# Merge gates of a decoder layer in seven block products instead of eight, product by product, with the sums of weight pieces on VectorE

## The chip, the cores and the metric

One NeuronCore of one Trainium2 chip. The metric is device time in microseconds of one execution; lower is better. TensorE is called PE here, VectorE DVE, ScalarE ACT, GpSimd POOL, and SP is the engine that issues most DMAs.

## The reference

One decoder layer on 1024 tokens of width 1024. What the change touches is the merge of two branches:

```python
qa, ka, va, qb, kb, vb, gb, gate_a, gate_b = jnp.split(h @ w_in[l], split_idx, axis=-1)
ya = oa.reshape(B, S, DA_WIDTH) @ w_branch_a[l]
yb = (jax.nn.silu(gb) * ob) @ w_branch_b[l]
merged = jax.nn.sigmoid(gate_a) * ya + jax.nn.sigmoid(gate_b) * yb
x = x + merged @ w_out[l]
```

Ahead of it stand differential attention (4 heads) and retention (4 heads), behind it the output projection and a mixture of 32 experts.

## The kernel before

Every fp32 product is made of three: each operand is a high part (fp32r, an ACT copy) and a low part (value minus high part, a DVE subtraction), and `split3` (L109 to L115) issues high by high, low by high and high by low, each a matmul over 512 columns. The normed input stands turned in SBUF as `hTH[th]` and `hTL[th]` (high and low; th is the half of the tokens, 512 of them, and the 8 pieces k of 128 channels stand in each).

Four stages follow each other on PE. **Heads** (`head_steps`): four heads, each with 8 steps of attention (A) and 8 of retention (B) in a pipeline over token tiles. In the last steps of the last head (16 to 18), where no projection is left, `first_gates` (L640) fills 48 matmuls of the next stage in between: the gates of unit 0. **Gates and branches**: 16 units s, each a slab m = s % 8 of 128 output channels and a half th = s // 8 of the tokens. A unit is `gates(s)` (L815: 2 gates x 8 pieces x 3 matmuls) and `branches(s)` (L824: 2 branches x 4 pieces x 3). Its weights, 1.5 MB in four transfers (`load_C`, L502), go to one of two buffers `wC_in`; ACT copies them to `wCH` in three pieces of 128x1024 (`high_C`, L1046), DVE makes `wCL` (`low_C`, L1512). ACT then takes the tanh of both gates out of PSUM (L1211), DVE multiplies each by its branch (L1752) and adds the two (L1755) into `merged`. **Output projection**: 16 products of 24 matmuls each, with the router's small ones in between. **Experts**: 192 weight pieces of 1 MB, split by ACT and DVE.

Within an engine the order of the instructions is the order of the program text; engines wait for each other by semaphores only. Each engine has its own loop over the units. DVE's is: the three `low_C` of unit s + 1, then the three operations on unit s. POOL does nothing in the gate stage but one small product on the router's weights.

Of the kernel before, what the change touches and what calls it, by code (L numbers as in the profile page):

```python
# [8 lines left out]
ALU = mybir.AluOpType  # L9
# [46 lines left out]

MAGIC = 1.5 * 2.0 ** 23
# [51 lines left out]
def split3(pe, out, left, right, start, stop):  # L109


    (lh, ll), (rh, rl) = left, right
    pe.matmul(out, lh, rh, start=start, stop=False)  # L113
    pe.matmul(out, lh, rl, start=False, stop=False)  # L114
    return pe.matmul(out, ll, rh, start=False, stop=stop)  # L115


def decoder_layer(nc, T):
    with ExitStack() as ctx:
# [87 lines left out]
        oTH = sb("oTH", [P, 8, 512], F32R, at=oTH_at)  # L207
# [99 lines left out]
        def pick(t, c):  # L307
# [30 lines left out]
        slot_at = [R_HT, R_HT + 16 * KIB, R_WORK, R_B, R_B + 16 * KIB, R_OT, R_OT + 16 * KIB, merged_at[1],  # L338
                   R_HT + 32 * KIB, R_HT + 48 * KIB]
# [43 lines left out]
        def x_bank(i, half):  # L383
# [3 lines left out]
        names = """pos_in first_turned x_next wA_first late_in g1_in consts_in gains_in small_in x_again x_in0 x_in1 x_in2 x_in3 x_sq_done x_ms_done x_rstd_done  # L387
# [20 lines left out]
        PREP_C = {3: 0, 5: 1, 6: 2}  # L408
        PREP_T = {12: 0, 15: 1, 16: 2, 17: 3}
# [47 lines left out]
        def _(sp):  # L457
# [1582 lines left out]
```

## Time and profile before

| | |
|---|---|
| median of 3 runs | 1454.28 us (1452.56 to 1455.19) |
| span of the profiled execution | 1451.4 us |
| PE busy | 1423.0 us (98%), 7361 matmuls |
| DVE busy | 998.9 us (69%) |
| ACT busy | 827.7 us (57%) |
| POOL busy | 412.0 us (28%) |

The profile gives the span, from the first to the last instruction of the profiled execution; a time of that execution on the scale of the runs is not given apart from it. The median lies 2.9 us above the span. A matmul's recorded duration overlaps the next one's, so how fast PE goes is read from start to start.

### The profile page before, as it was taken

Reading aid. Unit: us, or ns where it says so; the run is one execution under the profiler, and the core shown is the slowest. Engines: PE = TensorE matmul, PEld = TensorE weight load, DVE = VectorE, ACT = ScalarE, POOL = GpSimd, SP = SyncE. Lnnn points to the kernel's source line nnn. Section 1 sums busy time; section 2 is a strip of 40 time slices with the busy share of each in tenths; the row PEclk is TensorE's granted clock in tenths of the full one; section 3 lists DMA queues with packets and bytes.
Section 4 is the critical chain, followed back from the end, with each engine's and each line's share of the span. In section 5 each row is a group of like instructions: output and inputs, shape, how many; then the busy total and the mean of one; then the engine's idle time right before and its main releaser. Section 6 shows DMA issues by size and latency. Waiting matters only on the chain.

```text
span 1451.4 us, 19659 instructions
## 1 busy us (share of the span) xinstructions
PE 1423.0 (98%) x7361; PEld 1203.3 (83%) x7362; DVE 998.9 (69%) x1440; ACT 827.7 (57%) x1349; POOL 412.0 (28%) x463
## 2 busy tenths in 40 slices
PE   6999999999999999999999999999999999999997
PEld 5888988988988888888888878888888888888885
DVE  7855754764664533435332558999999999999996
ACT  5643453453453322324233238888888888888883
POOL 3325324424424300000000112233333333333331
PEclk9999999999999999999999999999999999999999
DMA  5211110210210333463340549999999999999991
GB/s 178 56 45 35 28 44 2 62 44 1 63 45 1 88 87 88 114 167 88 87 183 6 216 168 421 405 384 386 386 388 382 398 383 402 399 393 404 398 405 52
DMA packets 132946, 285.94 MB, mean 197 GB/s; under 512 B 17897, under 2 KB 96881, under 8 KB 108274
## 3 DMA queue, kind: packets, MB, share of 16 engines
q1 hardware_dynamic: 119296, 263.58, 49.7%
q0 software_dynamic: 13248, 21.00, 3.9%
q8 instruction: 60, 0.98, 0.3%
q14 instruction: 36, 0.29, 0.1%
q10 hardware_dynamic: 306, 0.07, 0.0%
HBM read 286.70 MB, written 25.17 MB: 215 GB/s over the span
## 4 chain that ended last, share of the span: by engine, by line
PE 95%; DVE 2%; issue 1%; POOL 1%; DMA 0%; ACT 0%; POOLq 0%; SPq 0%; DVEq 0%
PE proj L113 18%; PE proj L115 18%; PE proj L114 18%; PE scores L113 7%; PE scores L115 7%; PE scores L114 7%; PE scores L719 2%; PE outs L796 2%; PE scores L588 2%; PE turned L113 1%; PE turned L115 1%; PE turned L114 1%; PE turned L588 1%; PE outs L890 1%; PE turned L759 1%
## 5 line engine op out<-in xcount | busy, mean ns | idle before, releaser
L1839 DVE TENSOR_TENSOR w_low<-w_slot,w_high 128x2048 fp32r<-128x2048 f32 x192 | 430.8, 2286 | 0.1
L1243 ACT ACTIVATE w_high<-w_slot 128x2048 fp32r<-128x2048 f32 x190 | 349.5, 1906 | 2.6 <-DMA w_slot<-in_w_up 2.6
L113 PE MATMUL proj<-w_high,xeH 128*128 128x512 f32 x512 | 202.1, 395 | 0.3 <-DVE xeL L1945 0.3
L115 PE MATMUL proj<-w_high,xeL 128*128 128x512 f32 x512 | 200.0, 391 | 0.0
L114 PE MATMUL proj<-w_low,xeH 128*128 128x512 f32 x512 | 199.6, 390 | 0.0
L1451 POOL DMA_INDIRECT out<-y,ids_rows x31 | 86.6, 2792 | 338.2 <-DVE y L1961 338.2
L1048 ACT ACTIVATE wCH<-wC_in 128x1024 fp32r<-128x1024 f32 x48 | 47.7, 1052 | 152.0 <-DMA wC_in<-in_w_branch_b 152.0
L1515 DVE TENSOR_TENSOR wCL<-wC_in,wCH 128x1024 fp32r<-128x1024 f32 x48 | 57.2, 1243 | 90.0 <-ACT wCH L1048 90.0
L115 PEld LDWEIGHTS proj<-w_high,xeL 128*128 128x128 f32 x512 | 96.1, 188 | 20.1
L113 PEld LDWEIGHTS proj<-w_high,xeH 128*128 128x128 f32 x512 | 96.6, 189 | 19.4 <-issue 0.4
L114 PEld LDWEIGHTS proj<-w_low,xeH 128*128 128x128 f32 x512 | 96.3, 188 | 19.1
L113 PE MATMUL proj<-wBH,hTH 128*128 128x512 f32 x256 | 111.9, 437 | 0.0
L115 PE MATMUL proj<-wBH,hTL 128*128 128x512 f32 x256 | 101.0, 395 | 0.0
L113 PE MATMUL proj<-wAH,hTH 128*128 128x384 f32 x256 | 98.6, 385 | 2.0 <-DVE wAL L1510 2.0
L114 PE MATMUL proj<-wBL,hTH 128*128 128x512 f32 x256 | 100.4, 392 | 0.0
L113 PE MATMUL scores<-w_high,hidH 128*128 128x512 f32 x248 | 99.7, 402 | 0.0
L115 PE MATMUL scores<-w_high,hidL 128*128 128x512 f32 x248 | 97.0, 391 | 0.0
L114 PE MATMUL scores<-w_low,hidH 128*128 128x512 f32 x248 | 96.7, 390 | 0.0
L115 PE MATMUL proj<-wAH,hTL 128*128 128x384 f32 x256 | 87.0, 340 | 0.0
L114 PE MATMUL proj<-wAL,hTH 128*128 128x384 f32 x256 | 86.7, 339 | 0.0
L1251 ACT ACTIVATE xs<-scores,small 128x128 f32<-128x128 f32 x256 | 70.0, 384 | 10.4 <-PE scores L588 6.1
L1439 POOL DMA_INDIRECT xe<-x_rows,ids_rows x32 | 59.5, 1860 | 24.2 <-DVE ids_rows L1862 9.6
(317 smaller groups left out, 3181.2 us busy)
## 6 DMA issues: line engine op xcount, KB each, us to landing
w_slot<-in_w_gate SPq DMA_DIRECT2D x64, 1024.0 KB, 8.1
w_slot<-in_w_up SPq DMA_DIRECT2D x64, 1024.0 KB, 8.0
w_slot<-in_w_down SPq DMA_DIRECT2D x64, 1024.0 KB, 7.8
wC_in<-in_w_in SPq DMA_DIRECT2D x32, 512.0 KB, 5.2
wB_in<-in_w_in SPq DMA_DIRECT2D x16, 512.0 KB, 6.4
wA_in<-in_w_in SPq DMA_DIRECT2D x9, 512.0 KB, 6.0
wC_in<-in_w_branch_a SPq DMA_DIRECT2D x16, 256.0 KB, 5.6
wC_in<-in_w_branch_b SPq DMA_DIRECT2D x16, 256.0 KB, 5.5
```

Source lines behind the costliest of these rows:

```text
L113: pe.matmul(out, lh, rh, start=start, stop=False)
L114: pe.matmul(out, lh, rl, start=False, stop=False)
L115: return pe.matmul(out, ll, rh, start=False, stop=stop)
L588: last = pe.transpose(dst[:, k * 128:(k + 1) * 128], src_rows[:, DS(k, 128, step=step)], ident)
L719: pe.matmul(SC[:, c, t0 * 128:t1 * 128], q_part[r, 0, :], k_part[r, 1 + t0:1 + t1, :].rearrange("p a b -> p (a b)"), start=q_part is qkTH ...
L1048: act.activation(wCH[sub][:, piece * 8:piece * 8 + 8, :], wC_in[sub][:, piece * 8:piece * 8 + 8, :], ACT.Copy).then_inc(S["wC_high"], 1)
L1243: act.activation(w_high[slot][:], w_in6[slot][:], ACT.Copy).then_inc(S["w_split"], 1)
L1251: act.activation(xs[:, k, :], SC[:, 0, k * 128:(k + 1) * 128], ACT.Copy, scale=g2x[:, k:k + 1]).then_inc(S["xs_done"], 1)
L1439: pool.indirect_dma_start(out=xe[j % 4][:], out_offset=None, in_=x2_dram, in_offset=ids_of(ids_rows, j), bounds_check=1023, oob_is_err=Fal ...
L1451: pool.indirect_dma_start(out=out_rows, out_offset=ids_of(ids_rows, j), in_=rows[:], in_offset=None, bounds_check=1023, oob_is_err=False). ...
L1515: dve.tensor_tensor(wCL[sub][:, r, :], wC_in[sub][:, r, :], wCH[sub][:, r, :].bitcast(F32), ALU.subtract).then_inc(S["wC_low"], 1)
L1839: dve.tensor_tensor(w_low[slot][:], w_in6[slot][:], w_high[slot][:].bitcast(F32), ALU.subtract).then_inc(S["w_lows"], 1)
```

## The change

The 2 x 8 x 2 gate products are regarded as one product of 2x2 blocks: the weights' blocks are (gate a, gate b) by (channels 0 to 511, 512 to 1023), the input's are (channels 0 to 511, 512 to 1023) by (tokens 0 to 511, 512 to 1023). Strassen's scheme computes the four result blocks from seven block products M1 to M7 in place of eight. Each is cut into 8 slabs m, so there are 56 products o of 4 pieces x 3 matmuls, listed in `GATE_PRODUCTS`: M5, M2, M1 with their 8 slabs each, then M3 and M6 in groups of four (M3 i, M3 i+1, M6 i, M6 i+1), then M4 and M7 the same way. Products 0 to 3 take the place of unit 0 in the last head. `branches` follow, all 16, each slab and half as before.

The weight operand of a product is the sum or difference of two blocks (M3 and M4: one block), made by DVE (`operand_sum(o)`, for the first six `early_sum(o)` inside the last head), with its high copy by ACT (`high_operand`) and its low part by DVE (`low_operand`). There are four buffers for operands and three for raw rows of 512 KB. The input operand is a block for M5 and M2, and a sum of blocks for the others: s1 for M1 is summed inside the last head (`sum_s1`), s3, s4, s6 and s7 in two halves each in the gate stage (`half_sum(u)` and `half_split(u)` on DVE, u = 0 to 7). Of such a sum POOL makes the sum of the low parts (`half_lows(u)`), DVE that of the high parts and then the sum of both. The results leave PSUM by ACT copies (M5, M2) or DVE additions (`add_product`: two for M1, one for the others); M6 and M7 are accumulated onto what their bank holds, which M3 or M4 left there. Buffers move: four weight buffers of 1 MB for the branches, `x2` and two of the experts' slots in other places.

```diff
+SINGLES, PAIRS = ("M5", "M2", "M1"), (("M3", "M6"), ("M4", "M7"))
+GATE_PRODUCTS = [(kind, m) for kind in SINGLES for m in range(8)]
+for _one, _two in PAIRS:
+    for _i in range(0, 8, 2):
+        GATE_PRODUCTS += [(_one, _i), (_one, _i + 1), (_two, _i), (_two, _i + 1)]
...
+ROW_OF = {"M5": 0, "M2": 8, "M1": 16, "M3": 24, "M6": 24, "M4": 32, "M7": 32}
+PLAIN = ("M3", "M4")
+BANK_OF = (1, 3, 4, 5, 0, 2, 6, 7)
+EARLY_SUMS, FILLED = 6, 4
...
+SUM_AT = {9: 0, 10: 1, 12: 2, 13: 3, 16: 4, 17: 5}
+S1_SUM_AT = {11: 0, 14: 1, 15: 2, 16: 3}
...
+            def load_gate(r):
...
+                pieces = (((GATE_A, 0), (GATE_A, 4)), ((GATE_B, 0), (GATE_B, 4)), ((GATE_A, 0), (GATE_B, 4)),
+                          ((GATE_A, 0), (GATE_B, 0)), ((GATE_B, 4), (GATE_A, 4)))[kind]
+                for j, (col, k) in enumerate(pieces):
+                    sp.dma_start(gate_raw[r % 3][:, j, :, :], w_in_v[:, k:k + 4, col + m * 128:col + m * 128 + 128]
+                                 ).then_inc(S[f"w_land{r % 3}"], DMA)
+
...
+            def gate_part(o, k):
+
+                (kind, m), slot = GATE_PRODUCTS[o], o % 4
+                high, low_ = right[kind]
+                added = kind in ("M6", "M7")
+                last = split3(pe, bank(BANK_OF[m]), (gate_high[slot][:, k, :], gate_low[slot][:, k, :]),
+                              (high[:, k, :], low_[:, k, :]), k == 0 and not added, k == 3, added)
+                if k == 3:
+                    last.then_inc(S["c_done"], 1)
+
+            first_pieces = [(o, k) for o in range(FILLED) for k in range(4)]
 
...
+            for o in range(FILLED, N_GATE):
+                kind, m = GATE_PRODUCTS[o]
...
+                if kind in ("M2", "M1"):
+                    pe.wait_ge(S["gate_out"], PLACE["M5" if kind == "M2" else "M2", m] + 1)
+                elif kind in ("M3", "M6", "M4", "M7"):
+                    before_it = {"M3": "M1", "M6": "M3", "M4": "M6", "M7": "M4"}[kind]
+                    pe.wait_ge(S["merged_step"], gate_adds(PLACE[before_it, m]))
...
+                    pe.wait_ge(S["h_low"], 4)
+                if m == 0 and kind in ("M3", "M4", "M6", "M7"):
+                    pe.wait_ge(S["h_low"], 4 + {"M3": 2, "M4": 4, "M6": 6, "M7": 8}[kind])
+                pe.wait_ge(S["wC_low"], o + 1)
+                for k in range(4):
+                    gate_part(o, k)
+                if o == 5:
+                    pe.wait_ge(S["t_free"], N_HEADS * T_ROUND - 1 + FREE)
...
+            def branches(s):
+                th, slot = s // 8, s % N_WC
+                tok = slice(th * 512, th * 512 + 512)
+                pe.wait_ge(S["wC_low"], N_GATE + s + 1)
+                if s < 4:
+                    pe.wait_ge(S["merged_step"], gate_adds(PLACE["M7", 2 * s + 1]))
+                else:
+                    pe.wait_ge(S["merged_step"], GATE_ADDS + 2 * (s - 4) + 2)
...
+            high_operand(6)
+            high_operand(7)
+            act.wait_ge(S["gTB"], 8 * N_HEADS + FREE)
+            act.activation(oT[:, N_HEADS + 3, 7 * 128:8 * 128], TB[:, 0:128], ACT.Copy, scale=0.25).then_inc(S["t_free"], 1)
+            for o in range(4):
+                copy_product(o)
+            for o in range(8, N_GATE):
+                if o - 4 < PLACE["M1", 0]:
+                    copy_product(o - 4)
+                high_operand(o)
+                if o in (9, 10, 12, 13, 16, 17, 30, 31):
+                    high_half((9, 10, 12, 13, 16, 17, 30, 31).index(o))
+                if o in (40, 42, 44, 46):
+                    high_turned((o - 40) // 2, 0)
+                if o >= 44 and o % 2 == 0:
+                    gate_tanh(0, (o - 44) // 2)
+            high_C(0)
+            high_C(1)
...
+            def half_lows(u):
+
+                s, ks = ("s3", "s4", "s6", "s7")[u // 2], slice(u % 2 * 2, u % 2 * 2 + 2)
...
+                    pool.wait_ge(S["h_low"], 4 + u % 2 + 1)
+                    pool.wait_ge(S["h_low"], 4)
+                    one, two, op = h_low["s1"], h_low["s3"], ALU.add
+                if s == "s7":
+                    pool.wait_ge(S["c_done"], PLACE["M2", 7] + 1)
...
+                pool.tensor_tensor(h_lows[s][:, ks, :], one[:, ks, :].bitcast(F32), two[:, ks, :].bitcast(F32), op
+                                   ).then_inc(S["h_lows"], 1)
+
+            for u in range(8):
+                half_lows(u)
...
+            def early_sum(o):
+
+                dve.wait_ge(S[f"w_land{o % 3}"], 2 * DMA * (o // 3 + 1))
+                if o >= 4:
+                    dve.wait_ge(S["c_done"], o - 3)
+                dve.tensor_tensor(gate_sum[o % 4][:], gate_raw[o % 3][:, 0, :, :], gate_raw[o % 3][:, 1, :, :], ALU.add
+                                  ).then_inc(S["h_step"], 1)
+
+            def low_operand(o):
+
+                (kind, m), slot = GATE_PRODUCTS[o], o % 4
+                whole = gate_raw[(ROW_OF[kind] + m) % 3][:, 0, :, :] if kind in PLAIN else gate_sum[slot][:]
+                dve.wait_ge(S["wC_high"], o + 1)
...
+            def sum_s1(k):
+
+                s = h_raw["s1"][:, k, :]
+                dve.tensor_tensor(s, b11[0][:, k, :].bitcast(F32), b22[0][:, k, :].bitcast(F32), ALU.add).then_inc(S["h_step"], 1)
+                for n, part in enumerate((b11[1], b22[1])):
+                    dve.wait_ge(S["h_step"], STEPS_TO[f"s1_{k}"] - 2 + n)
+                    dve.tensor_tensor(s, s, part[:, k, :].bitcast(F32), ALU.add).then_inc(S["h_step"], 1)
...
+            def half_sum(u):
+
+                s, ks = ("s3", "s4", "s6", "s7")[u // 2], slice(u % 2 * 2, u % 2 * 2 + 2)
...
+                raw = h_raw[s][:, ks, :]
+                dve.tensor_tensor(raw, one[:, ks, :].bitcast(F32), two[:, ks, :].bitcast(F32), op).then_inc(S["h_step"], 1)
+                dve.wait_ge(S["h_step"], S1_STEPS + 2 * u + 1)
+                dve.wait_ge(S["h_lows"], u + 1)
+                dve.tensor_tensor(raw, raw, h_lows[s][:, ks, :], ALU.add).then_inc(S["h_step"], 1)
+
+            def half_split(u):
+
+                s, ks = ("s3", "s4", "s6", "s7")[u // 2], slice(u % 2 * 2, u % 2 * 2 + 2)
...
+            def add_product(o):
+
+                kind, m = GATE_PRODUCTS[o]
+                a0, a1, b0, b1 = merged[0][:, m, :], merged[1][:, m, :], gateB[0][:, m, :], gateB[1][:, m, :]
+                dve.wait_ge(S["c_done"], o + 1)
+                if kind == "M1":
+                    dve.wait_ge(S["gate_out"], PLACE["M2", m] + 1)
+                    dve.tensor_tensor(a1, bank(BANK_OF[m]), a0, ALU.subtract).then_inc(S["merged_step"], 1)
+                    dve.tensor_tensor(b0, bank(BANK_OF[m]), b1, ALU.subtract).then_inc(S["merged_step"], 1)
+                    return
+                into = {"M3": a0, "M6": b0, "M4": b1, "M7": a1}[kind]
+                dve.wait_ge(S["merged_step"], 2 * m + 2)
+                dve.tensor_tensor(into, bank(BANK_OF[m]), into, ALU.add).then_inc(S["merged_step"], 1)
+
+            def operand_sum(o):
+
+                (kind, m), slot = GATE_PRODUCTS[o], o % 4
+                r = ROW_OF[kind] + m
+                dve.wait_ge(S[f"w_land{r % 3}"], 2 * DMA * (r // 3 + 1))
+                dve.wait_ge(S["c_done"], o - 3)
+                one, two = gate_raw[r % 3][:, 0, :, :], gate_raw[r % 3][:, 1, :, :]
+                if kind in ("M6", "M7"):
+                    dve.tensor_tensor(gate_sum[slot][:], two, one, ALU.subtract).then_inc(S["gate_sums"], 1)
+                else:
+                    dve.tensor_tensor(gate_sum[slot][:], one, two, ALU.add).then_inc(S["gate_sums"], 1)
...
+            operand_sum(6)
+            for o in range(6, N_GATE):
+                if o + 1 < N_GATE and GATE_PRODUCTS[o + 1][0] not in PLAIN:
+                    operand_sum(o + 1)
+                low_operand(o)
+                if o - 4 >= PLACE["M1", 0]:
+                    add_product(o - 4)
+                if o in (8, 9, 11, 12, 14, 15, 28, 29):
+                    half_sum((8, 9, 11, 12, 14, 15, 28, 29).index(o))
+                if o in (10, 11, 13, 14, 17, 18, 31, 32):
+                    half_split((10, 11, 13, 14, 17, 18, 31, 32).index(o))
+                if o in (41, 43, 45, 47):
+                    low_turned((o - 41) // 2, 0)
+            low_C(0)
+            low_C(1)
+            for o in range(N_GATE - 4, N_GATE):
+                add_product(o)
```

How the change moves DVE's program. Before, one unit in the second half (three low parts of the next unit, two multiplications, one addition, three low parts):

```order
L1515 TENSOR_TENSOR wCL0_108<-wC_in0_106,wCH0_110 128x1024 [waits wC_high] x3
L1752 SCALAR_TENSOR_TENSOR sig_116<-sig_116,scores 128x512 [waits ys_done,sig_tanh]
L1752 SCALAR_TENSOR_TENSOR sig_116<-sig_116,scores 128x512
L1755 TENSOR_TENSOR merged1_113<-sig_116 128x512 [waits merged_step]
L1515 TENSOR_TENSOR wCL1_109<-wC_in1_107,wCH1_111 128x1024 [waits wC_high] x3
```

Now, on DVE, from the sum of product 9 to the low part of product 10 (`s3_raw` and `s3L` are halves of the input sum s3; `gate_sum`, `gate_high`, `gate_low` are operands of weights):

```order
L1984 TENSOR_TENSOR gate_sum1_117<-gate_raw0_113 128x512 [waits c_done,w_land0]
L1699 TENSOR_TENSOR gate_low0_120<-gate_sum0_116,gate_high0_124 128x512 [waits wC_high]
L1948 TENSOR_TENSOR s3_raw_128<-hTH0_51 128x1024 [waits projB]
L1951 TENSOR_TENSOR s3_raw_128<-s3_raw_128,s3_lows_132 128x1024 [waits h_lows,h_step]
L1984 TENSOR_TENSOR gate_sum2_118<-gate_raw1_114 128x512 [waits c_done,w_land1]
L1699 TENSOR_TENSOR gate_low1_121<-gate_sum1_117,gate_high1_125 128x512 [waits wC_high]
L1948 TENSOR_TENSOR s3_raw_128<-hTH0_51 128x1024 [waits projB]
L1951 TENSOR_TENSOR s3_raw_128<-s3_raw_128,s3_lows_132 128x1024 [waits h_lows,h_step]
L1984 TENSOR_TENSOR gate_sum3_119<-gate_raw2_115 128x512 [waits c_done,w_land2]
L1699 TENSOR_TENSOR gate_low2_122<-gate_sum2_118,gate_high2_126 128x512 [waits wC_high]
L1957 TENSOR_TENSOR s3L_140<-s3_raw_128,s3H_136 128x1024 [waits h_high]
```

Between the two pieces for one product stand the halves of the input sums, whole 128x1024 operations. POOL, after its last step of the last head (before, the next row after `gatedR` was the router's `wr`):

```order
L1543 TENSOR_TENSOR gatedR_102<-onR_101,sg_96 128x128 [waits sg_done,gTB,gate_step]
L1585 TENSOR_TENSOR s3_lows_132<-hTL0_53 128x1024 [waits projB] x2
L1585 TENSOR_TENSOR s4_lows_135<-hTL1_54 128x1024 x2
L1585 TENSOR_TENSOR s6_lows_133<-s1L_146,s3L_140 128x1024 [waits h_low,h_step,c_done] x2
L1585 TENSOR_TENSOR s7_lows_134<-s4L_143,s1L_146 128x1024 [waits h_low,h_step,c_done] x2
L1592 TENSOR_TENSOR wr_172<-wr_172,g2_cols_174 128x288 [waits router_in]
```

Eight 128x1024 operations stand there, each of which a DVE addition waits for through `h_lows`. DVE again, from the low part of product 32 to the addition of product 30 (groups of M3 and M6; `proj0` and `proj1` are the banks of slabs 2 and 3):

```order
L1699 TENSOR_TENSOR gate_low0_120<-gate_raw1_114,gate_high0_124 128x512 [waits wC_high]
L1972 TENSOR_TENSOR merged0_105<-proj0,merged0_105 128x512 [waits merged_step,c_done]
L1957 TENSOR_TENSOR s7L_142<-s7_raw_130,s7H_138 128x1024 [waits h_high]
L1982 TENSOR_TENSOR gate_sum2_118<-gate_raw1_114 128x512 [waits c_done,w_land1]
L1699 TENSOR_TENSOR gate_low1_121<-gate_raw2_115,gate_high1_125 128x512 [waits wC_high]
L1972 TENSOR_TENSOR merged0_105<-proj1,merged0_105 128x512 [waits merged_step,c_done]
L1982 TENSOR_TENSOR gate_sum3_119<-gate_raw2_115 128x512 [waits c_done,w_land2]
L1699 TENSOR_TENSOR gate_low2_122<-gate_sum2_118,gate_high2_126 128x512 [waits wC_high]
L1972 TENSOR_TENSOR gateB0_109<-proj0,gateB0_109 128x512 [waits merged_step,c_done]
```

The sum of product 34 (`gate_sum2` in the fourth row, which waits for the end of product 30 by `c_done`) and the low part of product 33 now stand ahead of the addition of product 29 on `proj1`, for which PE waits through `merged_step` before it begins product 31 on the same bank.

## Rows read from the trace of the kernel before

**Rows 1.** The page: span, busy time of each engine, the chain's shares.
```profile
span 1451.4 us, 19659 instructions
...
PE 1423.0 (98%) x7361; PEld 1203.3 (83%) x7362; DVE 998.9 (69%) x1440; ACT 827.7 (57%) x1349; POOL 412.0 (28%) x463
...
PE 95%; DVE 2%; issue 1%; POOL 1%; DMA 0%; ACT 0%; POOLq 0%; SPq 0%; DVEq 0%
```

**Rows 2.** The waits of PE: released line, releaser; total us, times, longest.
```profile
PE scores L627 <- DVE x_all L1666: 5.4, 3, 3.8
```

**Rows 3.** Windows: busy us (instructions) of PE, PEld, DVE, ACT, POOL; clock; DMA share; GB/s.
```profile
492.30:742.70 250.40, 250.40 (x1106) 207.40 (x1106) 96.52 (x101) 71.56 (x86) 4.12 (x4) 1.00 0.37 98
...
900.00:950.00 50.00, 50.00 (x236) 41.85 (x235) 47.76 (x29) 43.15 (x42) 16.06 (x7) 1.00 1.01 405
```

**Rows 4.** The tile wCH: count, duration min/median/max in ns, first and last start.
```profile
L113 PE MATMUL proj<-hTH,wCH x128: 388/389/482, 479.4 to 720.3; 128*128 128x512 f32 x128
...
L113 PE MATMUL scores<-hTH,wCH x128: 388/389/390, 497.9 to 742.0; 128*128 128x512 f32 x128
```

**Rows 5.** Timeline of PE in the gate stage: start, us, instruction.
```profile
492.30 0.40 PE L113 MATMUL turned<-oTH,wCH 128*128 128x512 f32 x1
...
497.70 0.39 PE L115 MATMUL outs<-oTH,wCL 128*128 128x512 f32 x1
...
519.01 0.39 PE L113 MATMUL proj<-hTH,wCH 128*128 128x512 f32 x1
...
523.09 0.39 PE L113 MATMUL proj<-hTH,wCH 128*128 128x512 f32 x1
...
742.73 0.39 PE L113 MATMUL proj<-wDH,mergedH 128*128 128x512 f32 x1
```

**Rows 6.** Timeline of DVE, end of the last head and the gate stage.
```profile
469.12 1.22 DVE L1515 TENSOR_TENSOR wCL<-wC_in,wCH 128x1024 fp32r<-128x1024 f32 x1
...
475.72 1.51 DVE L1515 TENSOR_TENSOR wCL<-wC_in,wCH 128x1024 fp32r<-128x1024 f32 x1
...
491.33 1.22 DVE L1521 TENSOR_TENSOR oTL<-oT,oTH 128x1024 fp32r<-128x1024 f32 x1
...
498.23 0.69 DVE L1752 SCALAR_TENSOR_TENSOR sig<-sig,turned 128x512 f32<-128x512 f32 x1 [0.39 <-PE outs L115]
...
498.84 0.68 DVE L1752 SCALAR_TENSOR_TENSOR sig<-sig,outs 128x512 f32<-128x512 f32 x1
...
499.55 0.69 DVE L1755 TENSOR_TENSOR merged<-sig 128x512 f32<-128x512 f32 x1
...
506.74 3.50 DVE L1515 TENSOR_TENSOR wCL<-wC_in,wCH 128x1024 fp32r<-128x1024 f32 x3 [6.50 <-ACT wCH L1048]
```

**Rows 7.** Timeline of POOL, the same stretch, and its one large product at 623.6.
```profile
475.69 0.46 POOL L1389 TENSOR_TENSOR onR<-onR,gn_rows 128x128 f32<-128x128 f32 x1 [0.53 <-DVE onR L1624]
...
476.23 1.33 POOL L1391 TENSOR_TENSOR onR<-onR,gn_rows 128x128 f32<-128x128 f32 x1
...
623.62 1.77 POOL L1418 TENSOR_TENSOR wr<-wr,g_cols 128x288 f32<-128x288 f32 x1 [128.81 <-DMA small<-in_norm_g]
```

**Rows 8.** Timeline of DVE around 621.
```profile
621.37 3.50 DVE L1515 TENSOR_TENSOR wCL<-wC_in,wCH 128x1024 fp32r<-128x1024 f32 x3 [2.38 <-ACT wCH L1048]
```

**Rows 9.** Groups of POOL by form: count, busy us, mean ns.
```profile
L1395 POOL TENSOR_TENSOR gatedR<-onR,sg 128x128 f32<-128x128 f32 x32 | 15.6, 488 | 2.5
...
L1424 POOL TENSOR_TENSOR ms<-ms,ssq 128x1 f32<-128x1 f32 x8 | 1.5, 190 | 51.0 <-ACT x_sq L1218 51.0
```

**Rows 10.** Groups of ACT by form.
```profile
L1048 ACT ACTIVATE wCH<-wC_in 128x1024 fp32r<-128x1024 f32 x48 | 47.7, 1052 | 152.0 <-DMA wC_in<-in_w_branch_b 152.0
...
L1211 ACT ACTIVATE sig<-proj 128x512 f32<-128x512 f32 x16 | 8.7, 594 | 2.2 <-PE proj L115 2.2
```

**Rows 11.** Windows after the last output product, where the granted clock falls.
```profile
862.00:863.00 1.00, 1.00 (x6) 1.00 (x6) 0.86 (x7) 0.62 (x3) 0.00 (x0) 0.50 0.00 0
```

**Rows 12.** The page: DMA issues, KB each, median us to landing.
```profile
wC_in<-in_w_in SPq DMA_DIRECT2D x32, 512.0 KB, 5.2
```

More of the change, by code:

```diff
@@ L247, in decoder_layer @@
-        wD_at = [R_HT, R_B]
+        raw_at = [R_A, R_A + 4 * KIB, R_WORK + 16 * KIB]
+        gate_raw = [sb(f"gate_raw{i}", [P, 2, 4, 128], F32, at=raw_at[i]) for i in range(3)]
+        gate_sum = [sb(f"gate_sum{i}", [P, 4, 128], F32, at=R_A + (8 + 4 * i) * KIB) for i in range(4)]
+        gate_low = [sb(f"gate_low{i}", [P, 4, 128], F32R, at=R_A + (8 + 4 * i) * KIB) for i in range(4)]
+        gate_high = [sb(f"gate_high{i}", [P, 4, 128], F32R, at=R_A + (10 + 4 * i) * KIB) for i in range(4)]
@@ new lines, in _, with high_merged @@
+            high_C(0)
+            high_C(1)
+            gate_tanh(0, 6)
+            gate_tanh(0, 7)
+            def high_merged(i):
+                act.activation(mergedH[i // 4][:, :, i % 4 * 128:(i % 4 + 1) * 128], merged[i // 4][:, :, i % 4 * 128:(i % 4 + 1) * 128],
+                               ACT.Copy).then_inc(S["mH"], 1)
+            for s in range(N_UNITS):
+                if s + 2 < N_UNITS:
+                    high_C(s + 2)
+                if s == 0:
+                    act.wait_ge(S["c_done"], N_GATE)
+                if s < 4:
+                    high_turned(s, 1)
+                if s < 8:
+                    gate_tanh(1, s)
+                if s in (8, 9):
+                    high(wDH[0][s - 8][:], wD_in[0][:, (s - 8) * 4:(s - 8) * 4 + 4, :], S["w_land7"], DMA, S["wD_high"])
+                if s in (10, 11, 12, 13):
+                    act.wait_ge(S["sig_mul"], 8)
+                    high_merged(s - 10)
@@ L1213, in square_half @@
+            act.wait_ge(S["sig_mul"], N_UNITS)
+            for i in range(4, N_TILES):
+                high_merged(i)
             def square_half(cnt):
@@ L1747, in _ @@
-                if s == 0:
-                    dve.wait_ge(S["gated"], 8 * N_HEADS + FREE)
-                dve.wait_ge(S["sig_tanh"], 2 * s + 2)
-                dve.wait_ge(S["ys_done"], s + 1)
-                for g in range(2):
-                    dve.scalar_tensor_tensor(sig[:, g, :], sig[:, g, :], 1.0, bank(b0 + 2 + g), ALU.add, ALU.mult
+                m, th = s % 8, s // 8
+                if s + 2 < N_UNITS:
+                    low_C(s + 2)
+                if s < 4:
+                    low_turned(s, 1)
@@ new lines, in _ @@
+                if s in (9, 10):
+                    low(wDL[0][:, (s - 9) * 4:(s - 9) * 4 + 4, :], wD_in[0][:, (s - 9) * 4:(s - 9) * 4 + 4, :], wDH[0][s - 9][:],
+                        S["wD_high"], s - 8, S["wD_low"])
+                if s in (11, 12, 13, 14):
+                    low_merged(s - 11)
+                dve.wait_ge(S["gate_out"], 16 + 2 * s + 2)
+                dve.wait_ge(S["c_done"], N_GATE + s + 1)
+                for g, gate in enumerate((merged[th], gateB[th])):
+                    dve.scalar_tensor_tensor(gate[:, m, :], gate[:, m, :], 1.0, bank(BANK_OF[(2 * s + g) % 8]), ALU.add, ALU.mult
```

361 lines of the change are left out of this document (205 added, 156 removed).

## The prediction

> **What bounds the kernel now.** I read the page first: PE is busy for 98% of the span and is 95% of the chain that ended last [rows 1]. Busy time alone proves little, since matmuls overlap in the records, so the waits of PE come next: the longest, 5.4 us in all, is for the first tiles at the start [rows 2], and in the gate stage there is none. The windows say the same: from 492.3, where the first matmul after `first_gates` starts, to 742.73, where the output projection starts [rows 5], PE is busy throughout at a granted clock of 1.00 (2.4 GHz), while DVE works 96.5 us of 250.4, ACT 71.6 and POOL 4.1 [rows 3]. So PE's instructions are the bound there, and the others have room on average. The timeline gives the price of a matmul: 18 of them lie between the starts at 519.01 and 523.09 [rows 5], so 0.2267 us each; a block product of 12 takes 2.72 us. The experts' stage has PE full too [rows 3], and nothing in its program changes, so what is won or lost before it should reach the end.
>
> **Term 1, the matmuls removed.** Gates: 256 issues each of three kinds, 768 [rows 4]. After: 56 x 12 = 672. 96 x 0.2267 = **-21.8 us**. The 48 that are filled into the last head stay 48, so PE is at product 4 at 492.3 as now [rows 5]. If nothing else waited, product 17 would start at 492.3 + 13 x 2.72 = 527.7.
>
> **Prices on DVE and POOL.** A 128x512 of DVE takes 0.69, but the next can start 0.61 later (498.23 to 498.84) [rows 6]. A 128x1024 takes 1.22, with 1.14 from start to start: three in 3.50 [rows 6]. An operation that waits for its predecessor's result starts at its end (498.84 + 0.68, next at 499.55). POOL has no 128x1024 in the trace. Its sum of one column takes 0.19 and its product of 128 columns 0.49 at mean, 0.46 undisturbed [rows 7, 9], so 2.1 ns a column and 0.19 + 1024 x 0.0021 = 2.4 us. The product of 288 columns took 1.77 from 623.62, of which DVE's third piece of that moment ran until about 624.8 [rows 7, 8], which leaves 0.6 us for 288 columns; in proportion 0.6 x 1024 / 288 = 2.1. The lower bound is 1.3 (a line through 0.46 at 128 and 0.6 at 288), the upper 8 x 0.46 = 3.7. I take 2.1, from the largest operation.
>
> **What POOL's work costs DVE.** At 475.69 POOL starts a 0.46 us operation, at 475.72 DVE a 128x1024, which takes 1.51 instead of 1.22; POOL's next, begun at 476.23 beside it, takes 1.33 instead of 0.46 and ends just behind it [rows 6, 7]. Each is held up while the other runs, nearly for its whole length. So I charge DVE all of a POOL operation that meets a full DVE queue: 2.1 us each. The other reading, a fixed cost of 1.51 - 1.22 = 0.29 per POOL operation, is the lower bound. The Trainium skill (SBUF — State Buffer, Who interferes with whom) says that a DVE instruction with two SBUF inputs contends with a GpSimd one that reads SBUF, as an exclusive lock held for the whole instruction. By that rule eight operations cost DVE 8 x 2.1 = 16.8 us, by the fixed cost 2.3; it speaks against giving POOL these sums. The two rows agree with it.
>
> **Term 2, DVE in front of products 6 to 17.** The last piece that DVE does in the last head starts at 491.33 [rows 6]; two small ones take its place, so its loop over the products starts near 492.7, with products up to 5 prepared. Until the low part of product 17, which PE needs, it has: 13 sums and 12 low parts at 0.61, 15.3; six halves of input sums, each an addition and a second that waits for it, 1.22 + 0.04 + 1.14 = 2.40, 14.4; four low halves at 1.14, 4.6; eight POOL operations at 2.1, 16.8; and some 1.2 us at the start, since raw row 7 is fetched only after a sum in step 16 and lands 5.2 us later [rows 12] (an estimate). Sum 52.3, so 545.0 against PE's 527.7: PE is late by **+17.3 us**. All eight POOL operations fall there: the first four follow the last head at once, two follow the low halves of s3, and the last two wait only for product 15. The operands' four buffers cannot hide it: they hold DVE back when it is early, not the reverse. ACT's share here (a copy from PSUM, a high part, at times a 1.05 us half: at most 2.3 us per 2.72) fits [rows 10]. DMA fits too: 512 KB per 2.72 us, three rows ahead, landing in 5.2.
>
> **Term 3, PE behind an addition in the groups of M3/M6 and M4/M7.** In the second product of M6 (or M7) in each group PE accumulates on a bank that DVE's addition of M3 (or M4) must have read. In DVE's program that addition stands behind the sum for a product of the next group, which waits until PE has finished the very product before. So PE stops each time for: the end and the signal of its last matmul, 0.53 (497.70 to 498.23 [rows 5, 6]), the sum 0.61, the low part 0.61, the addition 0.69, some 0.05 for the signal, less the 0.23 after which PE would have gone on: 2.2 to 2.3 us. Eight groups, of which the last has no sum of a next group behind it: 7 x 2.2 = 15.4. Where ACT's or DVE's larger pieces stand ahead of an addition (before products 26, 30, 42, 46 and 54) I add 2.3 in all: **+17.7 us**. DVE has caught up by then: from product 18 to 23 it needs 4 x 0.61 = 2.4 per product against 2.72. Bounds: 1.4 per stop (only low part and addition behind PE's signal) and 2.7.
>
> **Edits at nothing.** The pieces inside the last head: a step there lasts longer than its DVE work, and the new ones (at most five 128x512, 3.4 us, in step 16) take the place of one 1.22 us piece; if a following step is pushed, up to +1.5 us. The branches alone: a unit of 24 matmuls is 5.44 us, DVE's share at most 1.14 + 2 x 1.14 + 1.9 = 5.3. Output projection: its first split weights and `merged` parts are made in units 8 to 14, before PE gets there. The x2 and experts' buffers have other places, but wait for the same events.
>
> **Sum.** -21.8 + 17.3 + 17.7 = +13.2. The profiled span would become 1451.4 + 13.2 = 1464.6, and the median 1454.3 + 13.2 = **1467.5 us**.
>
> **The rivals.**
> 1. POOL's operations cost DVE little (0.29 each, or 2.1 that fall into idle time). Then DVE has 52.3 - 16.8 + 2.3 = 37.8 us to do until 530.5; PE is late by 3, or by up to 6 where the halves come bunched: -21.8 + 4.5 + 17.7 = +0.4 to +2 and at most +3.5; about 1456. For it: POOL has waits of its own between its operations. Against: the two rows of 475.7.
> 2. It gets faster. The place is the addition in the groups: if it is out in time, because sums run ahead of the signals I charge, term 3 falls to a few tenths. With term 2 full that is -21.8 + 17.3 + 2 = -2.5 (1451.8); with rival 1 too, -21.8 + 4.5 + 2 = -15.3 (1439). It decides when the addition can be done 0.2 us after the product before. The order of the program speaks against it.
> 3. The clock. After the last output product PE did only small work with gaps, and the granted clock fell to 0.50 (1.2 GHz) at 862 [rows 11]. In the stretch before product 17 PE would work about 2.72 of each 4 us, with gaps of up to 4 us. A product at the lower level takes 5.44; against DVE's pace that loses up to 1.8 each, and three such products 5 us, outside the stretch 2.7 each: +13.2 + 5 to + 10, so 1473 to 1478. The Trainium skill (TensorE: Matmul & The Clock Gate, Part 1: The HAM clock gate) says that the clock goes to 1.2 GHz once PE has been idle and comes back with sustained work; by that rule the longest gaps could cost these 5 us, and without it nothing. I leave the clock out of the sum, since matmuls fill most of the stretch.
>
> **How the numbers follow.** Two tenths of a per cent, 2.9 us, is about what a measurement of this kernel tells from no change. Forecast (terms 2 and 3 both there): 0.65. Rival 1: 0.15, of which half stays within 0.2%. Rival 2: 0.04 on its slight side, 0.05 on its large side. Rival 3: 0.11. Slower by over 0.2%: 0.65 + 0.11 + 0.08 = 0.84. Within: 0.07 + 0.02 = 0.09. Faster: 0.02 + 0.05 = 0.07. The range: POOL at 1.3 takes 6.4 off (1461), stops of 1.4 another 5.6 (1455.5), which is also rival 1's middle; POOL at 3.7 adds 12.8 (1480), with a little clock 1483. So 1455 to 1483.
>
> **What would show it.** In the profile after: POOL rows of 128x1024 near 2.1 us or longer, DVE pieces of 128x512 that last 2 to 3 us between 495 and 545, and PE waits for `gate_low` before products 7 to 17, 15 to 20 us in all. Then seven PE waits of about 2.2 us for DVE's addition, every fourth product from 27 to 51, some 13 us apart. From the output projection on, all as before, 13 us later. It is wrong if PE shows no wait there, if the POOL rows don't lengthen DVE's, or if waits stand somewhere else, as at a DMA row or in the branches.

## The result, and the profile after

The changed kernel takes **1475.04 us** (median of 4 runs, 1473.78 to 1475.23) against 1454.58 (4 runs, 1452.56 to 1455.19): a ratio of 1.0142, 95% interval 1.0128 to 1.0157. It is slower by 20.5 us, where 13.2 were forecast.

The page of the changed kernel, span, busy times and the chain:

```profile
span 1473.3 us, 19883 instructions
...
PE 1414.3 (96%) x7265; PEld 1189.8 (81%) x7266; DVE 1108.3 (75%) x1592; ACT 849.2 (58%) x1401; POOL 431.7 (29%) x471
...
PE 89%; DVE 7%; issue 2%; ACT 1%; POOL 0%; DMA 0%; ACTq 0%; DVEq 0%; POOLq 0%
```

PE has 96 matmuls fewer than in [rows 1], and DVE has gone from 2% of the chain to 7%. The waits of PE (us in total, times, longest) say where:

```profile
PE scores L154 <- DVE gate_low L1699: 10.6, 5, 3.9
PE turned L154 <- ACT oT L1321: 5.9, 1, 5.9
PE scores L154 <- DVE merged L1972: 4.3, 3, 2.1
PE scores L154 <- DVE gateB L1972: 4.3, 3, 2.1
...
PE proj L154 <- DVE gateB L1972: 2.2, 2, 2.1
PE proj L154 <- DVE merged L1972: 2.2, 2, 2.1
PE outs L154 <- DVE merged L1972: 2.1, 1, 2.1
```

None of these stood in the gate stage before. The five groups for L1972, DVE's addition, hold seven stops of 2.06 us and four small ones. Windows over products 4 to 17, products 17 to 55 with their additions, and the branches (columns as in [rows 3]):

```profile
494.00:551.00 57.00, 41.58 (x159) 32.15 (x160) 54.69 (x47) 22.34 (x37) 23.41 (x11) 0.88 0.46 129
551.00:678.00 127.00, 111.22 (x470) 88.04 (x469) 81.58 (x121) 40.32 (x63) 1.43 (x1) 0.99 0.34 96
678.00:765.00 87.00, 87.00 (x385) 72.04 (x384) 59.68 (x70) 33.25 (x39) 0.00 (x0) 1.00 0.42 133
```

In the first, DVE is busy for 54.7 of 57 us: it is the bound there. In the second nobody is full, so what costs time is the order of the work. In the third PE is full again: the branches take 87.04 us, 384 matmuls at the forecast 0.2267.

The first window's POOL and DVE, side by side. Timeline of POOL:

```profile
496.34 10.66 POOL L1585 TENSOR_TENSOR s_lows<-hTL 128x1024 f32<-128x1024 f32 x4
520.62 2.62 POOL L1585 TENSOR_TENSOR s_lows<-s1L,s3L 128x1024 f32<-128x1024 f32 x1 [13.62 <-DVE s3L L1957]
527.55 2.57 POOL L1585 TENSOR_TENSOR s_lows<-s1L,s3L 128x1024 f32<-128x1024 f32 x1 [4.31 <-DVE s3L L1957]
544.58 5.37 POOL L1585 TENSOR_TENSOR s_lows<-s4L,s1L 128x1024 f32<-128x1024 f32 x2 [14.46 <-PE outs L156]
```

Timeline of DVE:

```profile
496.76 2.50 DVE L1699 TENSOR_TENSOR gate_low<-gate_sum,gate_high 128x512 fp32r<-128x512 f32 x1 [0.70 <-ACT gate_high L1157]
499.18 2.87 DVE L1711 TENSOR_TENSOR s1L<-s_raw,s1H 128x512 fp32r<-128x512 f32 x1
501.97 5.58 DVE L1984 TENSOR_TENSOR gate_sum<-gate_raw 128x512 f32<-128x512 f32 x2
507.47 0.68 DVE L1699 TENSOR_TENSOR gate_low<-gate_sum,gate_high 128x512 fp32r<-128x512 f32 x1
...
520.31 0.68 DVE L1984 TENSOR_TENSOR gate_sum<-gate_raw 128x512 f32<-128x512 f32 x1
520.91 2.88 DVE L1699 TENSOR_TENSOR gate_low<-gate_sum,gate_high 128x512 fp32r<-128x512 f32 x1
523.71 1.21 DVE L1948 TENSOR_TENSOR s_raw<-hTH 128x1024 f32<-128x1024 f32 x1
```

While POOL works, the same 128x512 of DVE takes 2.9 us instead of 0.68: each POOL operation (2.4 to 2.8 us) takes some 2.2 us from DVE. The loop's first sum starts at 501.97. Further on, DVE and PE at the first of the seven stops:

```profile
576.72 1.23 DVE L1951 TENSOR_TENSOR s_raw<-s_raw,s_lows 128x1024 f32<-128x1024 f32 x1
578.73 0.69 DVE L1982 TENSOR_TENSOR gate_sum<-gate_raw 128x512 f32<-128x512 f32 x1 [0.79 <-PE scores L156]
579.33 0.69 DVE L1699 TENSOR_TENSOR gate_low<-gate_raw,gate_high 128x512 fp32r<-128x512 f32 x1
579.94 0.69 DVE L1972 TENSOR_TENSOR merged<-scores,merged 128x512 f32<-128x512 f32 x1
```

```profile
578.23 0.39 PE L156 MATMUL scores<-s6H,gate_low 128*128 128x512 f32 x1
580.67 0.50 PE L154 MATMUL scores<-s6H,gate_high 128*128 128x512 f32 x1 [2.06 <-DVE merged L1972]
```

DVE itself is idle before the sum, which waits for PE's product 26; then sum, low part and addition follow, and only the last is what PE waits for.

### The profile page after: what moved, and what is told of

Read it like the earlier page. It is cut to its first block, busy times and chain, and to the rows that moved or that the text cites. A ratio compares the mean times of both kernels' runs of the same rounds, so it can differ in the third digit from the quotient of the medians.

```text
span 1473.3 us, 19883 instructions
## 1 busy us (share of the span) xinstructions
PE 1414.3 (96%) x7265; PEld 1189.8 (81%) x7266; DVE 1108.3 (75%) x1592; ACT 849.2 (58%) x1401; POOL 431.7 (29%) x471
## 4 chain that ended last, share of the span: by engine, by line
PE 89%; DVE 7%; issue 2%; ACT 1%; POOL 0%; DMA 0%; ACTq 0%; DVEq 0%; POOLq 0%
PE proj L154 17%; PE proj L156 17%; PE proj L155 17%; PE scores L154 6%; PE scores L156 6%; PE scores L155 6%; PE scores L813 2%; PE outs L890 2%; PE scores L670 2%; DVE gate_low L1699 2%; PE turned L154 1%; PE turned L156 1%; PE turned L155 1%; PE turned L670 1%; PE outs L988 1%
## 5 line engine op out<-in xcount | busy, mean ns | idle before, releaser
L1157 ACT ACTIVATE gate_high<-gate_sum 128x512 fp32r<-128x512 f32 x40 | 25.4, 635 | 87.6 <-DVE gate_sum L1982 53.2
```

## The experiments

Each ratio compares with runs of the kernel before on the same chip. These had medians of 1454.6 us beside the change, 1453.5 beside e1 to e4, 1454.0 beside e5 and e6 and 1452.5 beside e7 to e9, so a difference in us between kernels of two such groups is uncertain by 1 to 2 us. For the stretches, the starts of PE's products in each profiled execution: from product 4 to product 17 (PE alone: 13 x 2.72 = 35.4 us), and from product 17 to the branches' first matmul (39 x 2.72 = 106.1). In the ten profiled executions of changed kernels product 0 starts between 478.05 and 479.89 us, so a stretch is a better measure than a position.

```
kernel                    median us   ratio to before   products 4-17   17-branches
before                    1454.6      -                 -               -
the change                1475.0      1.0142            56.2            127.1
e1 additions first        1455.8      1.0014            56.2            107.6
e2 lows on VectorE        1469.2      1.0106            49.0            127.6
e3 lows as fills          1460.7      1.0044            41.9            128.2
e4 = e1 + e2              1450.2      0.9979            50.4            110.0
e5 = e4, spread           1450.5      0.9978            38.3            121.6
e6 = e5, one at a time    1435.9      0.9873            36.7            107.6
e7 = e6, lows on GpSimd   1443.9      0.9932            43.8            109.0
e8 = e6, additions back   1457.9      1.0029            36.7            129.3
e9 s1 of high parts only  1474.9      1.0144            53.9            130.7
```

**The additions put first.**

```diff
             for o in range(6, N_GATE):
+                if o - 4 >= PLACE["M3", 0]:
+                    add_product(o - 4)
                 if o + 1 < N_GATE and GATE_PRODUCTS[o + 1][0] not in PLAIN:
                     operand_sum(o + 1)
                 low_operand(o)
-                if o - 4 >= PLACE["M1", 0]:
+                if PLACE["M1", 0] <= o - 4 < PLACE["M3", 0]:
                     add_product(o - 4)
```

> The additions of products 24 to 51 are put ahead of the next weight sum on VectorE (nothing else moves). Theory (term 3: the stops at products 27, 31, ... 51 come from the addition standing behind a sum that itself waits for the bank): the seven stops of 2.06 us idle and the small ones go, 21.0 us between product 17 and the branches become 3 to 6; 1475.0 - 16 = 1459 us (1456 to 1462). Rival (VectorE is short of time there anyway, so the wait only changes its name): within 3 us of 1475.

1455.76 us (1454.04 to 1457.10, 11 runs), ratio 1.0014 (1.0005 to 1.0022): 19.3 us come back from an edit that moves one line, 3 more than expected and just outside the range given. The second stretch falls from 127.1 to 107.6 us, the first stays at 56.2. PE's waits there:

```profile
PE scores L154 <- DVE gate_low L1699: 10.6, 5, 3.9
PE turned L154 <- ACT oT L1321: 5.9, 1, 5.9
PE turned L714 <- DVE pos_rows_f L1900: 4.2, 1, 4.2
```

The waits for L1972 are gone from the top of the list, and the longest that is left is 0.5 us; the third row is one of the program's start. Term 3 holds, and the rival that VectorE would only rename the wait falls: VectorE had 127 - 82 = 45 us to spare there.

**The sums of low parts: on VectorE, and as fills.** In e2 `half_lows` is called by VectorE between the two additions of `half_sum`; GpSimd issues none. In e3 it stays on GpSimd but is a fill with zeros, so the sums of low parts are missing from its result:

```diff
-                pool.tensor_tensor(h_lows[s][:, ks, :], one[:, ks, :].bitcast(F32), two[:, ks, :].bitcast(F32), op
-                                   ).then_inc(S["h_lows"], 1)
+                pool.memset(h_lows[s][:, ks, :], 0.0).then_inc(S["h_lows"], 1)
```

> The eight sums of low parts move from GpSimd to VectorE, right behind the high parts' sum; GpSimd does none. Theory (lock: each 128x1024 sum of GpSimd costs VectorE 2.2 us, and one of its own costs 1.15): 8 x (2.2 - 1.15) = 8.4 us of VectorE's time comes back, less what lies beside idle time, so 1475.0 - 8 = 1467 us (1464 to 1471), and product 6 starts 4 to 5 us earlier. Rival (GpSimd costs VectorE little; rival 1 of the prediction): VectorE gets 8 x 1.15 more and the time is 1475 + 9 = 1484.

> GpSimd fills the eight low sums with zeros in place of adding (the low parts' sums are left out of s3, s4, s6 and s7). It issues as many instructions under the same waits, but reads nothing. Theory (VectorE is held while GpSimd reads two operands): VectorE's 128x512 ops beside the fills take 0.7 to 1.0 us, product 17 starts at 535 to 540, time 1475.0 - 15 = 1460 (1457 to 1464). Rival A (any GpSimd write holds VectorE for its whole length): each fill costs what it takes, 1 to 2 us, and the time is 1463 to 1472. Rival B (the delay is VectorE's own work): no change, 1475.

e2: 1469.19 us (1467.13 to 1470.86, 4 runs), ratio 1.0106 (1.0090 to 1.0123): VectorE has 9 us more operations and the kernel is 5.9 us faster. Its first stretch is 7.2 us shorter. e3: 1460.70 us (1459.10 to 1463.30, 6 runs), ratio 1.0044 (1.0032 to 1.0056), first stretch 14.2 us shorter. The timeline of POOL in e3, and DVE beside it:

```profile
495.94 3.63 POOL L1585 MEMSET s_lows<- 128x1024 f32 x4
```

```profile
496.37 0.69 DVE L1698 TENSOR_TENSOR gate_low<-gate_sum,gate_high 128x512 fp32r<-128x512 f32 x1 [0.70 <-ACT gate_high L1157]
496.98 0.68 DVE L1710 TENSOR_TENSOR s1L<-s_raw,s1H 128x512 fp32r<-128x512 f32 x1
497.58 1.29 DVE L1983 TENSOR_TENSOR gate_sum<-gate_raw 128x512 f32<-128x512 f32 x2
...
503.21 0.69 DVE L1983 TENSOR_TENSOR gate_sum<-gate_raw 128x512 f32<-128x512 f32 x1 [2.29 <-DMA gate_raw<-in_w_in]
```

Four fills of GpSimd run in 3.6 us, and VectorE's two-input operations beside them keep their 0.68 us. So GpSimd's writes don't hold VectorE up; the operation that reads two operands does. This hold-up is called the lock below. The Trainium skill (SBUF — State Buffer, Who interferes with whom) says that such a VectorE instruction contends with a GpSimd one that reads SBUF and not with one that only writes it; by these two kernels' rows (2.9 against 0.68 us) that holds.

**Both edits.** e4 is e1 and e2 together.

> Edits of e1 and e2 together. Theory (terms 2 and 3 are separate stretches and add): 1475.0 - 16 - 8 = 1451 us, a little more where VectorE's work at products 28 to 31 now bounds: 1453 (1449 to 1457), so level with the kernel before. Rival (VectorE's total is the bound and the two share one gain): 1460 or more.

1450.21 us (1449.08 to 1453.71, 12 runs), ratio 0.9979 (0.9970 to 0.9988). The two gains, 19.3 and 5.9, add to 25.2; measured are 24.8. The terms are separate, as the sum took them.

**The half sums spread.** Both kernels make s6 second instead of third, as products need it; e6 also takes a half sum's three operations apart.

```diff
-                s, ks = ("s3", "s4", "s6", "s7")[u // 2], slice(u % 2 * 2, u % 2 * 2 + 2)
+                s, ks = ("s3", "s6", "s4", "s7")[u // 2], slice(u % 2 * 2, u % 2 * 2 + 2)
...
-                if o in (8, 9, 11, 12, 14, 15, 28, 29):
-                    half_sum((8, 9, 11, 12, 14, 15, 28, 29).index(o))
+                for n, at in enumerate((7, 7, 8, 8, 9, 10, 13, 15, 16, 16, 16, 17,
+                                        19, 21, 28, 29, 32, 32, 33, 33, 36, 37, 37, 40)):
+                    if at == o:
+                        (half_sum, half_lows, half_join)[n % 3](n // 3)
```

(e6; `half_join` is the second addition; ACT's high parts follow at 10, 12, 16, 22, 28, 33, 39, 41, the splits at 12, 14, 18, 23, 29, 36, 40, 42. PE's and VectorE's counts of `h_low`, `h_high` and `h_step` follow the new order.)

> e4 with the half sums in the order s3, s6, s4, s7 (that in which they are needed) and spread: half_sum behind products 9, 11, 14, 17, 28, 30, 33, 35, ACT's high part one later, the split two later. Work is the same. Theory (between products 6 and 24 VectorE has about 1.5 us of slack a product, so what bounds is how many half sums stand ahead of a product, not their total): 2 instead of 3 half sums lie ahead of product 16 beyond the slack; 1450.2 - 4 = 1446 us (1443 to 1450). Rival (all of the rest is VectorE's total, order does nothing): 1450 or more, with the loss moved to products 28 to 39.

> e5 with each half sum's three operations apart, one or two of 1.15 us to a product, so that a product's add or low part never stands behind three in a row (3.7 us, more than a product's 2.72). Theory: the stretch from product 6 to the branches falls to PE's own 50 x 2.72 = 136 us plus 2 to 5 us of small stops, so out of e4's 1450.2 come 10 to 13 us: 1438 us (1434 to 1443), below the kernel before by 15. Rival (VectorE's total bounds, 8 x 4 x 1.15 = 37 us of half sums against its slack): 1445 or more.

e5: 1450.45 us (1447.93 to 1453.55, 12 runs), ratio 0.9978 (0.9969 to 0.9987): **a miss**, 4 us above what was expected and what the rival gave. The rival's reason holds in part: the first stretch gained 12.1 us (50.4 to 38.3), so order does do something, but the second lost 11.5, and the loss did move on. PE's waits in e5 show where.

```profile
PE scores L154 <- DVE merged L1970: 6.9, 2, 5.2
...
PE proj L154 <- DVE merged L1970: 2.6, 1, 2.6
```

And the timeline of DVE before that wait of 2.6:

```profile
578.13 0.69 DVE L1980 TENSOR_TENSOR gate_sum<-gate_raw 128x512 f32<-128x512 f32 x1 [2.31 <-PE proj L156]
578.74 0.69 DVE L1674 TENSOR_TENSOR gate_low<-gate_raw,gate_high 128x512 fp32r<-128x512 f32 x1
579.34 1.22 DVE L1945 TENSOR_TENSOR s_raw<-s4H,s1H 128x1024 f32<-128x1024 f32 x1
580.48 1.22 DVE L1925 TENSOR_TENSOR s_lows<-s4L,s1L 128x1024 f32<-128x1024 f32 x1
581.80 1.23 DVE L1949 TENSOR_TENSOR s_raw<-s_raw,s_lows 128x1024 f32<-128x1024 f32 x1
582.95 0.68 DVE L1970 TENSOR_TENSOR gateB<-proj,gateB 128x512 f32<-128x512 f32 x1
```

VectorE waits 2.3 us for PE, and then an addition stands behind three operations in a row, 3.6 us, which is more than the 2.72 of a product. The wait of 5.2, at product 34, has four large operations in a row ahead of the addition (585.95 to 590.68). Busy shares can't show this: VectorE is idle and late within one product. Some 3.9 of the 11.5 us is the clock (below): products 30 and 34 take 4.32 and 5.28 us instead of 2.85. The profiled execution is also e5's slowest, 3.1 us over the median. e6 takes such rows apart: 1435.93 us (1433.85 to 1436.02, 4 runs), ratio **0.9873 (0.9859 to 0.9888)**, with the same work as e5. Its windows over the three parts:

```profile
493.00:530.00 37.00, 36.49 (x159) 29.66 (x160) 35.46 (x46) 20.31 (x35) 1.72 (x3) 1.00 0.75 200
530.00:638.00 108.00, 107.70 (x472) 87.89 (x471) 91.81 (x129) 43.25 (x66) 4.74 (x1) 1.00 0.39 111
638.00:725.00 87.00, 87.00 (x386) 72.08 (x385) 59.66 (x71) 32.75 (x39) 0.00 (x0) 1.00 0.42 133
```

DVE is busy for 35.5 of 37 us in the first, and PE doesn't wait: it is full and in time. This version beats the kernel before by 18.0 us: -21.8 for the matmuls, +1.8 where PE waits ahead of product 4, and +1.3 and +1.5 left in the two stretches make -17.2; the spans of the two profiled executions differ by 17.3.

**Each repair taken back out of e6.** e7 gives the low sums back to GpSimd, e8 puts the additions back behind the sum.

> e6 with the sums of low parts back on GpSimd (as in the change), all else as in e6. Theory (lock, 2.2 us of VectorE each against 1.15 for doing it itself; the first four come in a row and stop VectorE at products 5 to 7): 1435.9 + 8 x (2.2 - 1.15) = 1444, up to 1448 with what the bunch costs. Rival (with the work well spread VectorE has slack for either, and taking 8 x 1.15 off it helps): 1434 to 1437.

> e6 with the additions back behind the next sum (as in the change). Theory (the stop of 2.06 us is made by the order alone and doesn't depend on how busy VectorE is): the seven stops at products 27, 31, ... 51 are back, 1435.9 + 19 = 1455 (1451 to 1460). Rival (the stops came from VectorE being late after the half sums): at most 5 us more, 1441.

e7: 1443.91 us (1442.34 to 1444.72, 4 runs), ratio 0.9932 (0.9916 to 0.9947): +8.0, where 8 x (2.2 - 1.15) is 8.4. e8: 1457.92 us (1454.70 to 1459.54, 6 runs), ratio 1.0029 (1.0015 to 1.0042): +22.0, with all seven stops of 2.06 back at products 27, 31, ... 51, though VectorE is never late in e6. Both rivals fall. So the stops are there in a smooth schedule as in the crowded one, and the lock costs the kernel 8.0 us here where e2 gained 5.9 by its removal. e8's excess over the 19 expected is the clock, below: in its profiled execution products 39 and 43 take 1.6 us each longer.

**The last head lightened.**

```diff
-                dve.tensor_tensor(s, b11[0][:, k, :].bitcast(F32), b22[0][:, k, :].bitcast(F32), ALU.add).then_inc(S["h_step"], 1)
-                for n, part in enumerate((b11[1], b22[1])):
-                    dve.wait_ge(S["h_step"], STEPS_TO[f"s1_{k}"] - 2 + n)
-                    dve.tensor_tensor(s, s, part[:, k, :].bitcast(F32), ALU.add).then_inc(S["h_step"], 1)
+                dve.tensor_tensor(s, b11[0][:, k, :].bitcast(F32), b22[0][:, k, :].bitcast(F32), ALU.add).then_inc(S["h_step"], 3)
```

> The change with s1 made of the high parts alone: the eight 128x512 operations of sum_s1 that add the low parts are left out of the last head (the low parts of s1 are missing from the result). Theory (the head's tail is not free as the prediction had it: its new operations on VectorE make the loop start 5 us later than forecast, and VectorE bounds up to product 17): 8 x 0.8 = 6.4 us less on VectorE, of which 3 to 5 reach product 17; 1475.0 - 4 = 1471 (1469 to 1473). Rival (VectorE waits for PE in the head, so its new work there is hidden and the loop's late start is the GpSimd operations' alone): 1475 within 1.

1474.92 us (1472.03 to 1475.08, 5 runs), ratio 1.0144 (1.0129 to 1.0159): no change in time, as the rival had it; for the theory this is a miss. But the rival's reason doesn't hold: counted from product 0, product 17 starts 4.1 us earlier than in the change (66.8 against 70.9), as the theory had it. The first 1.8 of it come at product 4, whose wait of 1.61 us for its low part is gone. Product 18 then waits 1.5 us for its low part, which leaves 2.3, and one product more than in the change runs at the low clock, 1.6 us; the branches start 0.4 us earlier. So head work on VectorE does reach PE, and what it gives was taken back further on. Whether the other runs lost it in the same way isn't known, as one execution is profiled.

## Why the prediction was right, and what was mis-sized

- **The direction, and Term 1.** Slower by over 0.2% had 0.84; the measured 1475.0 lies in 1455 to 1483, 7.5 us above the forecast. e6, where PE hardly waits, shows the 21.8 us of Term 1 to be real.
- **"Prices on DVE and POOL", "What POOL's work costs DVE".** POOL's operation was put at 2.1 us (1.3 to 3.7) and charged in full to DVE. Measured: 2.4 to 2.8 us, of which some 2.2 come off DVE. e2, e3 and e7 show it. Rival 1 is refuted. For the operation's length the 2.4 from the column rate was the better guide; that 2.1, charged in full, came out so near the 2.2 that DVE loses is in part luck.
- **Term 2, DVE in front of products 6 to 17: +17.3, measured +23.0** (product 17 at 550.65 instead of 527.7; 0.4 of it is a later start of the whole head). The term was mis-sized, in both directions. Between the change and e3 lie 14.2 us, which is what the eight POOL operations cost PE; 16.8 were charged. What stays without them is 8.4 (product 17 at 56.6 us from product 0; PE alone would need 12.9 + 35.4), where the sum had 0.5. The step that failed is **"edits at nothing", the pieces inside the last head**, and with it Term 1's remark that PE is at product 4 at 492.3: PE waits 1.61 us there for a low part, and product 4 starts at 494.47. Behind the 491.33 of [rows 6] I counted two small pieces; the trace has five and a wait for ACT, and what stands ahead of them runs 2 us late (DVE's last `onR` starts at 492.94 in e3, at 491.00 before). In e3 the loop starts at 497.58, 4.9 us behind the 492.7 of the prediction, with no POOL sum to blame. e9, with eight of these head operations left out, is at product 17 4.1 us earlier. The remaining 3 us aren't taken apart; DVE's wait of 2.29 us for a DMA in e3, where 1.2 were charged, is part of it. The first three of the five, in the timeline of DVE in e3 (the other two are its rows of 496.37 and 496.98 above), and PE's first matmul of product 4 in the change:

```profile
493.26 0.68 DVE L1698 TENSOR_TENSOR gate_low<-gate_sum,gate_high 128x512 fp32r<-128x512 f32 x1
493.86 0.94 DVE L1710 TENSOR_TENSOR s1L<-s_raw,s1H 128x512 fp32r<-128x512 f32 x1
494.73 0.95 DVE L1690 TENSOR_TENSOR gate_sum<-gate_raw 128x512 f32<-128x512 f32 x1
```

```profile
494.47 0.47 PE L154 MATMUL scores<-hTH,gate_high 128*128 128x512 f32 x1 [1.61 <-DVE gate_low L1699]
```

- **The wait for `oT`, 5.94 us, at product 6.** I had not forecast it by name. It is no separate cost: ACT's copy stands behind two high parts that wait for DVE's sums of 501.97 (5.58 us for two, under the lock), and in e2 and e3, without those, it is 0.37. Product 6's own low part ends at 508.15, 0.3 us before PE starts, so PE would have waited nearly as long for that.
- **Term 3: +17.7, measured 21.0.** The stop itself was right: 2.2 us charged, and from the start of one product to the next 4.94 instead of 2.72, so 2.22, seven times at the products named. Missing were 0.14 each for the first matmul after a stop (a product of 2.86), 1.0 in all; the clock, 1.5 (product 35); and 0.6 on the small stops, which came at the products named: 3.1 of the 3.3. e1 and e8 show the cause, twice.
- **Rival 3, the clock.** It was left out of the sum and came in part. Timeline of PE and windows in the change at product 35, ahead of which PE stood for 2.06 us:

```profile
607.63 0.80 PE L154 MATMUL scores<-s6H,gate_high 128*128 128x512 f32 x1 [2.06 <-DVE merged L1972]
608.22 0.63 PE L155 MATMUL scores<-s6L,gate_high 128*128 128x512 f32 x1
...
611.33 0.40 PE L154 MATMUL scores<-s6H,gate_high 128*128 128x512 f32 x1
```

```profile
607.60:612.00 4.40, 4.37 (x12) 3.51 (x13) 0.00 (x0) 0.00 (x0) 0.00 (x0) 0.62 0.40 117
622.40:625.30 2.90, 2.87 (x13) 2.38 (x14) 1.11 (x1) 0.38 (x1) 0.00 (x0) 1.00 0.60 177
530.80:535.90 5.10, 5.08 (x12) 4.04 (x13) 5.07 (x6) 2.55 (x4) 0.00 (x0) 0.50 0.21 59
```

  The granted clock is down to its lower level (1.2 GHz) for most of that product, which takes 4.40 us instead of 2.86. So it cost 1.5 us where the rival had 2.7: the clock was back before the product's end. The same stop before product 39 (second window) leaves the clock at 1.00. Product 12, after 3.9 us of idle time, takes 5.17 (third window). In the first stretch such products hide beside a VectorE that is full; in the second each costs 1.5 us.
- **Rival 2** (the addition in time) didn't happen in the change, but e1 makes it happen: 1455.8. The 1451.8 worked out for it lacked the 5.3 us by which Term 2 was too small.
- **Edits at nothing, the branches:** right, 87.04 us in the change and in all nine experiments, 384 matmuls at the price of before. From the output projection on nothing changed: it starts 22.05 us later, and the span grew by 21.9.

## What to carry to other kernels

An engine that is 64% busy can hold up PE seven times: look at what stands ahead of the operation that PE needs and what that one waits for in turn, before any busy share. Where an in-order queue holds work for later and work for now, what is needed now goes first, and what is not urgent goes in pieces shorter than one step of the engine that waits. Moving sums to an idle GpSimd was no relief for VectorE, which read SBUF at the same time: 2.2 us of VectorE were paid to save 1.15.

## What was unexpected of the hardware

- GpSimd's fill of 128x1024 takes 0.91 us (four in 3.63) and leaves VectorE at 0.68 us for a 128x512; its two-input sum of the same size takes 2.4 to 2.8 and lengthens one to 2.9.
- Of the seven stops, nearly all of 2.06 us, some are followed by a product at the lower clock and some not: one in the change (product 35), one in e2 (27, a stop of 2.35), one in e3 (51), two in e8 (39, 43), two in e9 (27, 39), at places that differ from kernel to kernel. In e4 it also came after stops of 1.84 and 1.80 us (products 13 and 16). A restart without it costs 0.14 us. So part of what a kernel's stops cost, 1.5 us a time, varies from kernel to kernel with the same stops; what decides it stays open. e6, in which PE has no stop over 0.4 us between products 5 and 56, shows the clock at 1.00 in all three of its windows.
